# A two-block layer on one core: three GEMM openings two tiles wide, loads in another order, and a third slot for split weights

## The reference, cut to what matters

```python
h = rmsnorm(x, mix_norm_g)
q, k, v, g, u = split(h @ w_in)                   # four heads of q, k, v, g; four pooling groups u
y_ret  = silu(g) * head_rmsnorm(retention(rope(q), rope(k), v), ret_gn_g)
y_pool = pool_mixer(u, pool_w, pool_scale)        # windows 2, 4, 8, 16
x = x + concat(y_ret, y_pool) @ w_out             # the first output projection
mem_n = rmsnorm(mem, mem_norm_g)
x = x + cross_attn(rmsnorm(x), mem_n, wq, wkv, wo)  # k, v = mem_n @ wkv
x = x + conv_glu_ffn(rmsnorm(x), w_up, conv_w, conv_b, w_down)
```

## Time and profile before

| | |
|---|---|
| median of 3 runs | 3088.25 us (3085.11 to 3093.66) |
| profiled execution | 3092.15 us, its span 3090.3 us |
| TensorE matmuls, busy | 2884.1 us (93%) |
| VectorE, ScalarE, GpSimd, busy | 50%, 26%, 34% |
| mean granted TensorE clock | 0.971 of full |

### The profile page before, as it was taken

The page is one execution under the profiler, slowest core; times in us unless marked ns, Lnnn a source line. Parts: engine busy times, 40 slices in busy tenths (PEclk is TensorE's granted clock), DMA queues, the critical chain, the costliest instruction groups (busy, mean ns, idle before and its releaser), DMA issues.

```text
span 3090.3 us, 35560 instructions
## 1 busy us (share of the span) xinstructions
PE 2884.1 (93%) x14278; PEld 2331.8 (75%) x14278; DVE 1539.8 (50%) x1903; ACT 802.4 (26%) x1137; POOL 1063.4 (34%) x473
## 2 busy tenths in 40 slices
PE   6999888989899999999988999999997999999996
PEld 5887677767788888888767888888775777777774
DVE  7334514122666665566845555666537444444434
ACT  4221212231200000000243334444323333333331
POOL 4232366214344444444412122222236333333223
PEclk9999999999999999999989999999998899999998
DMA  3111222001111111111211122222121111111112
GB/s 129 35 35 35 103 81 69 28 21 48 36 47 48 48 48 48 48 48 48 95 49 57 58 64 65 65 65 65 51 96 75 35 35 35 35 43 40 35 35 109
DMA packets 94228, 170.26 MB, mean 55 GB/s; under 512 B 30192, under 2 KB 56976, under 8 KB 93968
## 3 DMA queue, kind: packets, MB, share of 16 engines
q1 hardware_dynamic: 86272, 140.00, 14.1%
q10 hardware_dynamic: 7312, 26.28, 2.2%
q0 software_dynamic: 512, 2.07, 0.2%
HBM read 149.39 MB, written 18.94 MB: 54 GB/s over the span
## 4 chain that ended last, share of the span: by engine, by line
PE 79%; DVE 11%; issue 3%; ACT 3%; POOL 3%; DMA 2%; POOLq 0%; ACTq 0%; DVEq 0%; SPq 0%
PE gemm L523 17%; PE gemm L525 17%; PE gemm L524 17%; PE small L613 3%; PE small L524 3%; PE small L523 3%; PE small L525 3%; PE small L1122 2%; PE small L1144 2%; PE small L989 1%; PE small L1132 1%; DVE norm L1816 1%; POOL xres L501 1%; PE small L639 1%; DVE xres L2570 1%
## 5 line engine op out<-in xcount | busy, mean ns | idle before, releaser
L523 PE MATMUL gemm<-h_hi,w_hi 128*128 128x512 f32 x2688 | 1141.0, 424 | 79.3 <-DVE h_lo L1826 23.5
L525 PE MATMUL gemm<-h_hi,w_lo 128*128 128x512 f32 x2688 | 1072.9, 399 | 0.0
L524 PE MATMUL gemm<-h_lo,w_hi 128*128 128x512 f32 x2688 | 1072.7, 399 | 0.0
L456 POOL TENSOR_TENSOR w_hi<-w_raw,unit_col 128x1024 fp32r<-128x1024 f32 x174 | 343.6, 1975 | 1598.1 <-PE gemm L525 1447.2
L523 PEld LDWEIGHTS gemm<-h_hi,w_hi 128*128 128x128 f32 x2688 | 514.6, 191 | 200.5 <-issue 61.1
L525 PEld LDWEIGHTS gemm<-h_hi,w_lo 128*128 128x128 f32 x2688 | 511.6, 190 | 123.9
L524 PEld LDWEIGHTS gemm<-h_lo,w_hi 128*128 128x128 f32 x2688 | 514.8, 192 | 105.6 <-issue 6.5
L458 POOL TENSOR_TENSOR w_lo<-w_raw,w_hi 128x1024 fp32r<-128x1024 f32 x174 | 467.7, 2688 | 13.7
L492 POOL TENSOR_TENSOR w_hi<-w_raw,unit_col 128x1024 fp32r<-128x1024 f32 x32 | 61.4, 1920 | 362.0 <-PE gemm L525 361.9
L2085 DVE TENSOR_TENSOR norm<-gemm,norm 128x1024 f32<-128x1024 f32 x44 | 53.9, 1226 | 192.1 <-PE gemm L525 189.8
L525 PE MATMUL small<-act_hi,w_lo 128*128 128x512 f32 x352 | 139.2, 396 | 0.0
(11 more groups left out here) (381 smaller groups left out, 3748.2 us busy)
## 6 DMA issues: line engine op xcount, KB each, us to landing
w_raw<-w_stream SPq DMA_DIRECT2D x206, 512.0 KB, 3.2
x_spill<-xres ACTq DMA_DIRECT2D x16, 512.0 KB, 2.6
xres<-x_t SPq DMA_DIRECT2D x8, 512.0 KB, 13.0
xres<-x_t ACTq DMA_DIRECT2D x8, 512.0 KB, 9.3
xres<-g_rows SPq DMA_DIRECT2D x8, 512.0 KB, 3.9
...
```

The costliest lines, as they stand in the source:

```text
L456: nc.gpsimd.tensor_tensor(whi[s][:, :, :], raw[s][:, :, :], unit, ALU.mult).then_inc(w_hi_done, 1)
L523: mm(dst, w_hi, a_hi, start=first, stop=False)
L524: mm(dst, w_hi, a_lo, start=False, stop=False)
L525: return mm(dst, w_lo, a_hi, start=False, stop=last)
```

## The change

1. Launch: the first two tiles are a `gemm_pair`; the norm's sums and spread move from s = 28 and 31 to 36 and 39, so into tile 2. VectorE makes the low slices and sums of squares before the position angles, and the cosine is taken from the folded sine. SyncE loads tile 1's weights after the first slice of x, GpSimd issues all loads but the vector table after the first two splits.
2. Output projection: tiles x 0 and x 1 are a `gemm_pair`. The low slices 0 to 3 stand in front of the last pooling tree. x is reloaded earlier, in two parts, and the memory norm's sum stands after the pair instead of after x 2.
3. A third slot of split weights, `w_hi2` and `w_lo2`, in the 8 KB behind `mem_lo`, is used by the 24 tiles of `MIX_OUT` in turn with the two others (i % 3). The raw slots stay two. A split in it waits for the tile three back. The first one waits for the low slices of the output projection, since `yt` lies there. Squares of the cross attention's norm move from `yt` to `norm`.
4. Feed-forward: the first two tiles are a `gemm_pair` with the norm's sums and spread among it; VectorE takes the sum of square 6 behind seven low slices.

```diff
--- before.py
+++ after.py
@@ -151,8 +151,11 @@
             pass
         with nc.sbuf_tensor("memx", [P, KT, N_MEM], F32) as memx, \
                 nc.sbuf_tensor("mem_hi", [P, KT, N_MEM], F32R) as mem_hi, \
-                nc.sbuf_tensor("mem_lo", [P, KT, N_MEM], F32R) as mem_lo:
+                nc.sbuf_tensor("mem_lo", [P, KT, N_MEM], F32R) as mem_lo, \
+                nc.sbuf_tensor("w_hi2", [P, KT, P], F32R) as w_hi2, nc.sbuf_tensor("w_lo2", [P, KT, P], F32R) as w_lo2:
             pass
+        whi.append(w_hi2)
+        wlo.append(w_lo2)
...
@@ -346,7 +349,7 @@
 
             if j == NMEM:
                 return H[:, 0, (k % 2) * N_MEM:(k % 2 + 1) * N_MEM]
-            return yt[:, 6 + k % 2, :] if j == NXA else N[:, k % 2, :]
+            return N[:, 2 + k % 2, :] if j == NXA else N[:, k % 2, :]
...
-            for t in range(2):
-                sp.dma_start(raw[t][:, :, :], w_stream[t]).then_inc(w_loaded[t], 16)
-                if t == 0:
-                    for k in range(KT):
-                        sp.dma_start(xres[:, k, :], x_t[k]).then_inc(x_loaded[k], 16)
+            sp.dma_start(raw[0][:, :, :], w_stream[0]).then_inc(w_loaded[0], 16)
+            for k in range(KT):
+                if k == 1:
+                    sp.dma_start(raw[1][:, :, :], w_stream[1]).then_inc(w_loaded[1], 16)
+                sp.dma_start(xres[:, k, :], x_t[k]).then_inc(x_loaded[k], 16)
...
@@ -444,23 +447,24 @@
...
+            def split_slot(t, s, turn, into=None):
+
+                d = s if into is None else into
+                pool.wait_ge(w_loaded[s], 16 * turn)
+                nc.gpsimd.tensor_tensor(whi[d][:, :, :], raw[s][:, :, :], unit, ALU.mult).then_inc(w_hi_done, 1)
+                pool.wait_ge(w_hi_done, t + 1)
+                nc.gpsimd.tensor_tensor(wlo[d][:, :, :], raw[s][:, :, :], whi[d][:, :, :].bitcast(F32),
+                                        ALU.subtract).then_inc(w_split, 1)
+
+            pool.wait_ge(eps_set, 2)
+            split_slot(0, 0, 1)
+            split_slot(1, 1, 1)
             pool.dma_start(H[:, 3, :].bitcast(I32), positions.broadcast_to([P, S])).then_inc(pos_loaded, 16)
...
             nc.gpsimd.tensor_tensor(small_lo[:, :, :], small_raw[:, :, :], small_hi[:, :, :].bitcast(F32),
                                     ALU.subtract).then_inc(small_split, 1)
 
-            with pool.Fori(1, T_FOX // 2) as i:
+            def split_pair(i):
+
                 for s in range(2):
-
                     pool.wait_ge(pe_slot, 2 * i + s - 1)
                     split_slot(2 * i + s, s, i + 1)
+
+            with pool.Fori(1, T_WOUT // 2) as i:
+                split_pair(i)
+            for i in range(len(MIX_OUT)):
+                t = T_WOUT + i
+                if i == 2:
+
+                    pool.wait_ge(h_lo_done, KT * (HRET + 1))
+                if i != 2:
+                    pool.wait_ge(pe_slot, t - 1 if i < 2 else t - 2)
+                split_slot(t, t % 2, t // 2 + 1, i % 3)
+            with pool.Fori(T_XQ // 2, T_FOX // 2) as i:
+                split_pair(i)
 
...
@@ -524,16 +541,16 @@
...
-            def gemm_tile(t, b, a_hi, a_lo, width, fresh=None, among=None, s0=0):
...
+            def gemm_tile(t, b, a_hi, a_lo, width, fresh=None, among=None, s0=0, held=None):
+
+                d = b if held is None else held
                 pe.wait_ge(w_split, t + 1)
...
-                        last = dot3(gp[b][:, c:c + w], whi[b][:, k, :], wlo[b][:, k, :],
+                        last = dot3(gp[b][:, c:c + w], whi[d][:, k, :], wlo[d][:, k, :],
                                     a_hi[:, k, c:c + w], a_lo[:, k, c:c + w], k == 0, k == KT - 1)
...
@@ -687,11 +704,11 @@
             def ret_among(w):
 
                 def at(s):
-                    if w == 0 and s == 28:
+                    if w == 0 and s == 36:
...
                         token_sums(pa[:, 0:NB], N[:, 2, :]).then_inc(norm_mm, 1)
-                    if w == 0 and s == 31:
+                    if w == 0 and s == 39:
...
@@ -706,16 +723,17 @@
...
-                for j in range(4):
+                if w == 0:
+                    gemm_pair(T_RET, hhi, hlo, HMIX, among)
+                for j in range(0 if w else 2, 4):
                     t = T_RET + 4 * w + j
-                    if t >= 2:
-
-                        pe.wait_ge(tile_out, t - 1)
-                    gemm_tile(t, t % 2, hhi, hlo, S, HMIX if t == 0 else None, among, 16 * j)
+
+                    pe.wait_ge(tile_out, t - 1)
+                    gemm_tile(t, t % 2, hhi, hlo, S, None, among, 16 * j)
...
-                if s == 2 * (KT - 1) - 1:
+                if s == 19:
                     pool_product(3)
...
-                if kind == "x":
-                    gemm_tile(t, t % 2, hhi, hlo, S, HRET if i == 0 else None, pool_last if i == 0 else None)
+                if i == 0:
+                    gemm_pair(T_WOUT, hhi, hlo, HRET, pool_last)
+                elif i == 1:
+                    continue
+                elif kind == "x":
+                    gemm_tile(t, t % 2, hhi, hlo, S, held=i % 3)
                 else:
-                    gemm_tile(t, t % 2, mem_hi, mem_lo, N_MEM, HMEM if m == 0 else None)
-                if i == 2:
+                    gemm_tile(t, t % 2, mem_hi, mem_lo, N_MEM, HMEM if m == 0 else None, held=i % 3)
+                if i == 0:
...
@@ -845,16 +867,19 @@
...
 
             pe.wait_ge(tile_added, 2 * KT)
-            for q in range(4):
-                if q >= 2:
-                    pe.wait_ge(tile_out, EV_FF + q - 1)
-                gemm_tile(T_FF + q, q % 2, hhi, hlo, S, HFF if q == 0 else None)
-                if q == 1:
-
+            def ff_start(s):
+
+                if s == 25:
                     pe.wait_ge(sq_added, KT * (NFF + 1))
                     token_sums(pa[:, 0:NB], N[:, 2, :]).then_inc(norm_mm, 1)
+                if s == 28:
                     pe.wait_ge(norm_rstd, S_FF + 1)
                     spread(pa, R_H).then_inc(norm_wide, 1)
+
+            gemm_pair(T_FF, hhi, hlo, HFF, ff_start)
+            for q in range(2, 4):
+                pe.wait_ge(tile_out, EV_FF + q - 1)
+                gemm_tile(T_FF + q, q % 2, hhi, hlo, S)
...
@@ -1283,6 +1308,7 @@
...
+            act.wait_ge(sq_added, KT * (NMIX + 1))
...
                         A(N[:, 1, :], yt[:, g, :], ACT.Square).then_inc(y_squared, 1)
+                        if w == RET:
+                            for k in range(5):
+                                act.dma_start(xres[:, k, :], x_t[k]).then_inc(x_loaded[k], 16)
...
                     if k == KT - 1:
+                        act.wait_ge(h_lo_done, KT * HRET + 2)
+                        act.dma_start(memx[:, :, :], mem_t).then_inc(mem_loaded, 16)
                         pool_scaled(3)
+                        for n in range(5, KT):
+                            act.dma_start(xres[:, n, :], x_t[n]).then_inc(x_loaded[n], 16)
                     act.wait_ge(pool_y, k - RET + 1)
                 A(hhi[:, k, :], yt[:, k, :], ACT.Copy).then_inc(h_hi_done, 1)
-
-            act.wait_ge(h_lo_done, KT * (HRET + 1))
-            act.dma_start(memx[:, :, :], mem_t).then_inc(mem_loaded, 16)
-            for k in range(KT):
-                act.dma_start(xres[:, k, :], x_t[k]).then_inc(x_loaded[k], 16)
...
@@ -1855,37 +1883,33 @@
...
+            for k in range(KT):
+                dve.wait_ge(h_hi_done, KT * HMIX + k + 1)
+                V.scalar_tensor_tensor(hlo[:, k, :], xres[:, k, :], vc("mix_g", k), hhi[:, k, :].bitcast(F32), ALU.mult,
+                                       ALU.subtract).then_inc(h_lo_done, 1)
+            for k in range(KT):
+                add_square(NMIX, k)
             dve.wait_ge(pos_loaded, 16)
             done(V.tensor_copy(yt[:, 5, :], H[:, 3, :].bitcast(I32)))
...
-            for dst, shift in ((SIN, 0.0), (COS, 0.25)):
-                done(V.tensor_scalar(yt[:, 4, :], yt[:, 5, :], 1.0 / (2 * math.pi), shift, ALU.mult, ALU.add))
+            done(V.tensor_scalar(yt[:, 4, :], yt[:, 5, :], 1.0 / (2 * math.pi), None, ALU.mult))
+            settle()
+            done(V.tensor_scalar(yt[:, 4, :], yt[:, 4, :], ROUND_MAGIC, ROUND_MAGIC, ALU.add, ALU.subtract))
+            settle()
+            dve.wait_ge(norm_root, NMIX + 1)
+            V.reciprocal(R_H, R_H).then_inc(norm_rstd, 1)
+            done(V.scalar_tensor_tensor(SIN, yt[:, 4, :], -TWO_PI_HI, yt[:, 5, :], ALU.mult, ALU.add))
+            settle()
+            for part in (TWO_PI_MID, TWO_PI_LO):
+                done(V.scalar_tensor_tensor(SIN, yt[:, 4, :], -part, SIN, ALU.mult, ALU.add))
                 settle()
-                done(V.tensor_scalar(yt[:, 4, :], yt[:, 4, :], ROUND_MAGIC, ROUND_MAGIC, ALU.add, ALU.subtract))
...
-                done(V.tensor_scalar(dst, dst, shift * 2 * math.pi, math.pi, ALU.add, ALU.min))
-                settle()
-                if shift:
-                    V.tensor_scalar(dst, dst, -math.pi, None, ALU.max).then_inc(angles, 1)
```

(16 more changed lines are left out.)

30 lines of the change are left out of this document (3 added, 27 removed).

## The result

The changed kernel took 3062.12 us (median of 4 runs, 3059.93 to 3063.57) beside 3090.95 for the kernel before: a ratio of 0.9908, 95% interval 0.989 to 0.9926, or 28.8 us. Run again later beside the experiments it took 3062.14 (5 runs), ratio 0.9898 (0.9882 to 0.9914). The forecast was 3046 with a range up to 3064. Direction and range held, but 45 us were forecast and 29 to 32 came.

What follows compares the result with a forecast made beforehand. TensorE was taken as the bound, its matmuls busy 2884 of 3090 us, leaving about 200 us of waits. Gains 6 - 0.9 + 11.1 + 18.8 + 6.6 + 3.5 = 45.1 gave 3046 us, range 3034 to 3064.

Steps and rivals of the forecast that it cites:

- Launch: Kernel start to head 0's key transposes: low slices before angles start TensorE earlier; gain 6 us, bounds 3 and 9.
- Head 3: Five x loads on ScalarE between square and root of the last head: cost 0.9 us, bounds 0 and 2.
- Opening: First output projection up to memory tile 0: earlier low slices and the pair gain 11.1 us, bounds 8 and 14.
- Memory stretch: Memory tile 0 to end of x tile 7: third slot lets splits start earlier; gain 18.8 us, bounds 15 and 19.5.
- Tail: After x tile 7, four memory tiles up to the next projection: gain 6.6 us, bounds 4 and 10.4.
- feed-forward: Feed-forward opening: earlier low slices, sums inside the pair, third tile's split late; gain 3.5 us, bounds 1 and 5.
- Rival 1: Engine overlap makes all memory stretch splits take 6.1 us; stretch gives 5, total about 3060 us; chance 0.10.
- Rival 2: Launch gives nothing, rotated keys stay the stop at 78.6 us; total 3053 us; chance 0.10.
- Rival 3: Short waits hold TensorE's clock at 1.2 GHz from 349 to 456; slower, 3135 us; chance 0.03.
- Rival 4: New waits of pairs, ScalarE loads and raw loads give gains back; about 3084 us, no difference; chance 0.03.
- Its signs: Trace marks: key transposes at 69 to 74, x-to-x time 20.4 to 21, next projection near 465 to 470 us.

Runs made afterwards that it cites:

- e5: The changed kernel with tile 5's split at launch held until both rotations of head 0 are done: 3056.7 us, one run.
- e3: The kernel before with the third slot of split weights alone, no pair and no moved load: 3067.86 us, ratio 0.9918.
- e1: The changed kernel with GpSimd's split for output projection tile 3 waiting until the eight memory squares are summed: 3050.64 us, ratio 0.9852.
- e2: The changed kernel with the eight memory squares and their sums moved into idle time before low slice 7: 3050.48 us, ratio 0.9854.
- e4: The changed kernel with two slots of split weights instead of three, splits waiting for the tile two back: 3075.12 us, ratio 0.9941.
- e7: The changed kernel itself, run again beside the other experiments: 3062.14 us, ratio 0.9898.
- e8: The changed kernel with VectorE's low slices and GpSimd's splits taking turns by order before the cross attention: 3064.39 us, one run.

## Why the prediction was right, and where it was not

**The sum as a whole.** The forecast had 45.1, the traces have 29.5. Of the 15.6 that are missing 8.7 lie in the opening of the output projection, 2.5 at launch, 1.8 in the memory stretch, 1.6 in a clock that the sum had at nothing, and 1 in the rest. The time stayed 2 us inside the range because the range reached down to the sum of all lower bounds (3063). The sum of the upper ones is 57.9, not 57.

**Launch, 3.5 for 6.** TensorE started at 11.94 (forecast near 12) and tile 2 at 40.53 (forecast 40.5). The failing part is the list of VectorE. The sums over features stood on TensorE at 45.65, as forecast, but the prediction let the angles go on at that time: the sums take 1.8 us, the root then passes ScalarE and VectorE, and the reciprocal came at 47.89, only 0.7 before that of the kernel before (48.62). And the overlap cost about 6 us (2.4 at the products, 3.8 at the second rotation) where the sum left some 5. "That ends near 71" was 75.1, beyond the 73.5 of its lower bound. e5 shows the share of the second rotation: 4.0. How much of the 3.5 is the change's own is not shown: e3, whose launch is that of the kernel before, was at 77.50.

**Head 3, -1.0 for -0.9: the number by luck.** The five loads were to cost 0.9, but from the key transposes of head 3 (249.52 and 246.65) to the pooling product (284.47 and 281.60) it took 34.95 us in both kernels: they cost nothing. The 1.0 arises elsewhere, 0.7 behind the transposes of head 0 and 0.4 in the last pooling tiles, with a granted clock of 0.96 and 0.90 where it was 0.97 and 0.92.

**Opening, 2.4 for 11.1: the step that failed** is "which VectorE does after eight memory squares (5 us from 343.1)". Everything up to it held: 3.16 wait (forecast 3.2), slice 7 low at 339.1 (343.0 less the 2.5 of shift is 340.5), pair done at 343.7 (346.5 less 2.5 is 344.0). The squares' 5 us fit the kernel before, where no split lay beside the sums. The prediction itself named the overlap of the two engines, but for instructions of 1024 columns; it put the third slot's split only up to 349 and did not see that the splits of tiles 3 and 4, which wait for the two tiles of the pair, would follow it at once. The runs put in its place: 14.4 us from 339.05, the start of the first of the eight, to the first sum into `xres` at 353.41. Tile 2 came 7.8 us later than forecast by this, and the matmuls at half clock make up the other 0.9. e1 takes two of the three splits away, e2 takes the sums away, e4 the back to back order, and each time the wait goes to 2.84 us or less. That rests on one profiled execution of each; the wait of 9.7 itself stands in four, the changed kernel, e7, e5 and e8.

**Memory stretch, 17.0 for 18.8**, and alone (e3) with the tail 22.9: mechanism right and size nearly. The period is 21.1 us (388.92, 410.11, 431.04, 452.25 are starts of x tiles) where 20.7 was forecast: an x tile took 11.35 us instead of 11.2, and the next one began at T + 9.76 instead of T + 9.5, its split having ended at T + 9.6. TensorE waits 1.2 us for it and not 0.3, but that costs nothing more: it was ready at T + 8.5 and not 9.2, since a memory tile is shorter than the 3.08 that the forecast took from a busy time. ScalarE's evacuations of the memory tiles show it, 2.85 us apart:

```profile
382.03 0.39 ACT L1278 ACTIVATE norm<-gemm 128x256 f32<-128x256 f32 x1 [0.51 <-PE gemm L542]
384.90 0.38 ACT L1278 ACTIVATE norm<-gemm 128x256 f32<-128x256 f32 x1 [2.48 <-PE gemm L542]
387.73 0.38 ACT L1278 ACTIVATE norm<-gemm 128x256 f32<-128x256 f32 x1 [2.45 <-PE gemm L542]
```

**Tail, 6.1 for 6.6, feed-forward, 3.0 for 3.5.** Right. The feed-forward's third tile waits 3.56 us for its split, which the forecast had as the late one, and follows the first by 30.4 (forecast 29 to 31):

```profile
778.27 0.47 PE L540 MATMUL gemm<-h_hi,w_hi 128*128 128x512 f32 x1 [3.56 <-POOL w_lo L458]
```

**The rivals.** Rival 1 (overlap eats the third slot) had the right mechanism in the wrong place: the stretch's splits stayed at 1.9 + 2.4 us but for the one beside VectorE's two instructions (3.27 for w_lo), and it was VectorE's small sums before the stretch that paid. That its 3060 lies near the measured time is chance: its stretch was to give 5, and 17.0 came. Rival 2 is half true (3.5 of the launch's 6 came, and by e3 it may be less). Rival 3 did not happen: from 379 to 464 the granted clock was 1.00, and the cold stretch of 4.5 us lay behind the 9.7 us wait. Rival 4 did not happen either, though tile 2 did wait 3.24 us behind the launch's pair. The Trainium skill's rule on shared interfaces (GPSIMD Engine Reference, Specifications), weighed in the prediction, bears on the failed step: the trace agrees with it, and shows in numbers that a short instruction pays as much as a long one: 0.52 went to between 2.0 and 2.5 us, 1.22 to 2.94 and 3.35.

**Its signs.** Three of the places that it named were missed by a little: the transposes (75.1, named 69 to 74), the period (21.1, named 20.4 to 21) and the next projection (481.4, named 465 to 470), the last because of opening and launch.
